# Encoder trunk on one core: last tile of the first scale vector, place of the small transfers, square-root table, zeroing of an accumulator

## The reference

```python
cond = jax.nn.silu(c)
for i in range(DEPTH):
    mod = (cond @ ada_w[i] + ada_b[i])[:, None, :]
    sh1, sc1, g1, sh2, sc2, g2 = jnp.split(mod, 6, axis=-1)
    h = rmsnorm(x, norm_w[i, 0]) * (1 + sc1) + sh1
    h = gated_deltanet(...) if i % 2 == 0 else conformer_conv(...)
    x = x + (1 + g1) * rmsnorm(h, norm_w[i, 1])
    h = rmsnorm(x, norm_w[i, 2]) * (1 + sc2) + sh2
    h = swiglu(h, ffn_in_w[i], ffn_out_w[i])      # (silu(gate) * up) @ out_w
    x = x + (1 + g2) * rmsnorm(h, norm_w[i, 3])
```

## Time and profile before

| | |
|---|---|
| median of three runs | 3267.35 us (3266.91 to 3268.53) |
| profiled execution, its own time | 3268.26 us |
| its span in the profile | 3266.7 us |
| busy share of the span | TensorE 90%, VectorE 69%, ScalarE 39%, GpSimd 5% |
| mean granted TensorE clock | 0.95 |
| HBM traffic | 730 MB, 224 GB/s over the span |

### The profile page before, as it was taken

The page is one execution under the profiler, slowest core; times in us unless marked ns, Lnnn a source line. Parts: engine busy times, 40 slices in busy tenths (PEclk is TensorE's granted clock), DMA queues, the critical chain, the costliest instruction groups (busy, mean ns, idle before and its releaser), DMA issues.

```text
span 3266.7 us, 37727 instructions
## 1 busy us (share of the span) xinstructions
PE 2953.7 (90%) x13796; PEld 2382.1 (73%) x13796; DVE 2264.2 (69%) x2388; ACT 1275.6 (39%) x1383; POOL 163.6 (5%) x313
## 2 busy tenths in 40 slices
PE   1699999997777698899999999799987999999998
PEld 1577778876777577788888888644576888888886
DVE  6588868967776478787877877529966655555555
ACT  2356634335554334333333333421144333333333
POOL 0011111320111000000000000000000000000000
PEclk8799999998998799999999999899998999999998
DMA  9666766674332598798888888354334766656653
GB/s 376 227 224 238 244 218 217 206 235 146 104 104 65 182 372 327 274 341 308 310 308 315 337 315 333 99 167 149 122 121 155 252 206 216 201 201 203 214 204 122
DMA packets 322173, 731.61 MB, mean 224 GB/s; under 512 B 48128, under 2 KB 64336, under 8 KB 293648
## 3 DMA queue, kind: packets, MB, share of 16 engines
q1 hardware_dynamic: 316256, 709.85, 61.5%
q0 software_dynamic: 5808, 20.35, 1.8%
HBM read 710.45 MB, written 19.69 MB: 224 GB/s over the span
## 4 chain that ended last, share of the span: by engine, by line
PE 82%; DVE 7%; DMA 4%; ACT 3%; issue 2%; POOL 2%; DVEq 0%; SPq 0%; ACTq 0%
PE psg L664 44%; PE psg L670 22%; PE psg L651 5%; DMA aring<-in_ada_w 3%; PE psn L925 2%; PE pst L641 1%; PE psn L691 1%; PE psg L864 1%; DVE wlo L1086 1%; PE psg L885 1%; PE psn L1049 1%; DVE y L1598 1%; PE psn L641 1%; DMA wraw<-in_gdn_out_w 1%; PE pst L856 1%
## 5 line engine op out<-in xcount | busy, mean ns | idle before, releaser
L1722 ACT ACTIVATE whi<-wraw 128x2048 fp32r<-128x2048 f32 x408 | 781.8, 1916 | 1319.7 <-PE psg L670 1163.6
L1086 DVE TENSOR_TENSOR wlo<-wraw,whi 128x2048 fp32r<-128x2048 f32 x408 | 935.2, 2293 | 482.9 <-ACT whi L1722 481.0
L664 PE MATMUL psg<-whi,h_hi 128*128 128x512 f32 x2304 | 731.3, 399 | 33.6 <-DVE h_lo L1678 13.2
L664 PE MATMUL psg<-whi,h_lo 128*128 128x512 f32 x2304 | 719.9, 394 | 0.0
L670 PE MATMUL psg<-wlo,h_hi 128*128 128x512 f32 x2304 | 572.1, 391 | 12.0 <-DVE wlo L1086 12.0
L664 PEld LDWEIGHTS psg<-whi,h_hi 128*128 128x128 f32 x2304 | 435.5, 191 | 127.9 <-issue 25.6
L670 PEld LDWEIGHTS psg<-wlo,h_hi 128*128 128x128 f32 x2304 | 433.6, 188 | 104.0 <-DVE wlo L1086 13.9
L664 PEld LDWEIGHTS psg<-whi,h_lo 128*128 128x128 f32 x2304 | 439.5, 191 | 93.9
L1096 DVE SCALAR_TENSOR_TENSOR aacc<-aring,cond,aacc 128x2048 f32<-128x2048 f32 x150 | 352.0, 2346 | 6.6 <-DMA aring<-in_ada_w 6.0
L651 PE MATMUL psg<-wraw,aring 128*128 128x512 f32 x512 | 221.1, 592 | 0.0
L664 PE MATMUL psg<-whi,g_hi 128*128 128x512 f32 x704 | 219.9, 394 | 0.0
(11 more groups left out here) (251 smaller groups left out, 2600.0 us busy)
## 6 DMA issues: line engine op xcount, KB each, us to landing
aring<-in_ada_w SPq DMA_DIRECT2D x192, 1024.0 KB, 7.0
wraw<-in_ffn_in_w SPq DMA_DIRECT2D x176, 1024.0 KB, 6.8
wraw<-in_gdn_in_w SPq DMA_DIRECT2D x96, 1024.0 KB, 5.1
wraw<-in_ffn_out_w SPq DMA_DIRECT2D x88, 1024.0 KB, 5.2
wraw<-in_cf_pw_w SPq DMA_DIRECT2D x48, 1024.0 KB, 5.5
wraw<-in_gdn_out_w SPq DMA_DIRECT2D x32, 1024.0 KB, 8.5
wraw<-d_rr SPq DMA_DIRECT2D x16, 1024.0 KB, 4.7
x<-in_x SPq DMA_DIRECT2D x2, 2048.0 KB, 9.2
```

The costliest lines, as they stand in the source:

```text
L664: mm(ps[:, t, 0:width], a[:, kc, t * P:(t + 1) * P], wh, start=first and j + n == 0, stop=False)
L1086: tt(wlo[:, j % 2, :], wraw[:, j % 4, :], whi[:, j % 2, :].bitcast(F32), SUB).then_inc(w_lo, 1)
L1722: av(whi[:, j % 2, :], wraw[:, j % 4, :], ACT.Copy).then_inc(w_hi, 1)
```

## The change

Five edits. (1) TensorE first sums `aacc` of the scale (16 matmuls), then multiplies tile 31 into a place of its own in another PSUM bank (16 matmuls); VectorE adds the bias to the first sum and then adds the second. (2) `wba` and `alog` are loaded between the second and third weight tile of qkv, and `gwb` behind the fourth; none stands between the tiles of `ada_w` any more. (3) Factor 1/D and epsilon go into ScalarE's root as its scale and bias; the two VectorE steps and one semaphore wait disappear, and the first half's root comes ahead of the second half's square. (4) `root_table` is a root of one element into `scr` that nobody reads: it stands in front of the last block of a stage, and `out_root` moves in front of the next weight tile's `hi`. At an FFN's end VectorE multiplies blocks 0 to 2 by their weights before block 3 has come. (5) The zeroing of `y` becomes a ScalarE copy with scale 0 behind the third `hi` of the FFN.

```diff
@@ SyncE, opening
             for a in range(4, 2 * KC):
                 load_ada0(a)
-                if a == 16:
-                    for j in range(4):
-                        sp.dma_start(gwb[:, j, :], gdn_norm_w[0].partition_broadcast(P)).then_inc(gw_land, 16)
-                    for n, src in enumerate((gdn_A_log, gdn_dt_bias)):
-                        sp.dma_start(alog[:, n, :], src[0].rearrange("a b -> (a b)").partition_broadcast(P)).then_inc(c_land, 16)
-                if a == 20:
-                    sp.dma_start(wba.rearrange("p (j n) -> p j n", n=P),
-                                 gdn_in[:, QKV + VD:QKV + VD + P].rearrange("(j p) n -> p j n", p=P)).then_inc(wba_land, 16)
...
-            load_qkv(0)
+            for j in range(4):
+                load_w(G_QKV + j, (G_QKV + j) % 4, rows4(gdn_in, j * KT * P, 0))
+                if j == 1:
+                    sp.dma_start(wba.rearrange("p (j n) -> p j n", n=P),
+                                 gdn_in[:, QKV + VD:QKV + VD + P].rearrange("(j p) n -> p j n", p=P)).then_inc(wba_land, 16)
+                    for n, src in enumerate((gdn_A_log, gdn_dt_bias)):
+                        sp.dma_start(alog[:, n, :], src[0].rearrange("a b -> (a b)").partition_broadcast(P)).then_inc(c_land, 16)
+                if j == 2:
+                    load_ada(32, aring, (0, 2), 0)
+            for j in range(4):
+                sp.dma_start(gwb[:, j, :], gdn_norm_w[0].partition_broadcast(P)).then_inc(gw_land, 16)
             load_qkv(1)
@@ TensorE, opening
             for kc in range(KC):
-                if kc == 0:
-                    pe.wait_ge(a0_land[last % 4], 16 * (last // 4 + 1))
-                i = mm(psn[:, 0, kc:kc + 1], aring0[:, last % 4, kc * P:(kc + 1) * P], cond[:, KC - 1:KC], start=True, stop=False)
-                if kc == KC - 1:
-                    i.then_inc(a_used, 1)
-                i = mm(psn[:, 0, kc:kc + 1], aacc[:, 1, kc * P:(kc + 1) * P], ones[:, 0:1], start=False, stop=True)
+                i = mm(psn[:, 0, kc:kc + 1], aacc[:, 1, kc * P:(kc + 1) * P], ones[:, 0:1], start=True, stop=True)
             i.then_inc(a_fin, 1)
+            pe.wait_ge(a0_land[last % 4], 16 * (last // 4 + 1))
+            for kc in range(KC):
+                i = mm(psn[:, 2, kc:kc + 1], aring0[:, last % 4, kc * P:(kc + 1) * P], cond[:, KC - 1:KC], start=True, stop=True)
+            i.then_inc(a_used, 1)
@@ VectorE, pre and post
-                    dve.wait_ge(sq_ok, TT * n + t + 1)
                     r = st[:, 2 * n, t:t + 1]
-                    ts(r, r, 1.0 / D, RMS_EPS, MUL, ADD).then_inc(ms_ok, 1)
                     dve.wait_ge(rt_ok, TT * n + t + 1)
...
-                dve.wait_ge(yr_ok, 3 * n + 1)
-                ts(r, r, 1.0 / D, RMS_EPS, MUL, ADD).then_inc(yr_ok, 1)
                 post_col(n, 3, yb, cw)
@@ VectorE, opening
-            mod_add(2, 1)
+            dve.wait_ge(a_fin, 2)
+            tt(vec[:, NV_C:NV_C + KC], psn[:, 0, 0:KC], vec[:, NV_ADAB + KC:NV_ADAB + 2 * KC], ADD).then_inc(half_ok, 1)
+            dve.wait_ge(half_ok, 1)
+            dve.wait_ge(a_used, 2 * KC)
+            tt(mod[:, 1, :], psn[:, 2, 0:KC], vec[:, NV_C:NV_C + KC], ADD).then_inc(mod_ok, 1)
@@ VectorE, ffn
-                nc.vector.memset(y[:, :, :], 0.0).then_inc(y_zero, 1)
-                dve.wait_ge(y_zero, f + 1)
...
+                dve.wait_ge(y_zero, f + 1)
                 with dve.Fori(0, (GRP - 1) // 2) as i:
...
                     if j == 2:
                         dve.wait_ge(cw_land, 16 * (2 * f + 2))
-                        post_col(2 * f + 1, 0, y, cwb)
-                post_col(2 * f + 1, 1, y, cwb)
-                post_col(2 * f + 1, 2, y, cwb)
+                        for n in range(3):
+                            post_col(2 * f + 1, n, y, cwb)
@@ ScalarE, squares
                 for t in range(TT):
                     act.wait_ge(*ready(t))
-                    if n or t:
-                        act.wait_ge(sq_ok, TT * n + t)
                     av(dump, x[:, t, :], ACT.Square, accum_out=st[:, 2 * n, t:t + 1]).then_inc(sq_ok, 1)
-                for t in range(TT):
-                    act.wait_ge(ms_ok, TT * (n - 1) + t + 1)
-                    av(st[:, 2 * n, t:t + 1], st[:, 2 * n, t:t + 1], ACT.Sqrt).then_inc(rt_ok, 1)
+                    act.wait_ge(sq_ok, TT * n + t + 1)
+                    av(st[:, 2 * n, t:t + 1], st[:, 2 * n, t:t + 1], ACT.Sqrt, scale=1.0 / D, bias=epsr[:, 1:2]).then_inc(rt_ok, 1)
...
+            def root_table():
+                av(scr[:, :], epsr[:, 2:3], ACT.Sqrt)
@@ ScalarE, ahead of FFN 0 (ahead of FFN 1 alike)
             hi(G_F0, G_F0)
+            root_table()
             y_evac(3)
             out_squares(0, 3, yg, dump0[:, :], (ps_read, S_F0))
+            out_root(0)
             hi(G_F0 + 1, G_F0 + 1)
-            out_root(0)
@@ ScalarE, ffn
+                    if j == 2:
+                        av(y[:, :, :].rearrange("p t d -> p (t d)"), ident[:, 0:1].broadcast_to([P, TT * D]), ACT.Copy, scale=0.0
+                           ).then_inc(y_zero, 1)
...
                 hi(gl + 2, g0 + 2)
+                root_table()
                 hi(gl + 3, g0 + 3)
```

More of the change, by code:

```diff
@@ L134, in build @@
         epsr = sb("epsr", [P, 3])
+        scr = sb("scr", [P, 1])
         alog = sb("alog", [P, 2, 64])
@@ L283, in build @@
         xt_ok = sem("xt_ok")
-        wba_land = sem("wba_land")
+        wba_land, half_ok = sem("wba_land"), sem("half_ok")
         ba_done, ba_T, ba_tr = sem("ba_done"), sem("ba_T"), sem("ba_tr")
@@ L290, in build @@
         sq_ok = sem("sq_ok")
-        ms_ok = sem("ms_ok")
         rt_ok = sem("rt_ok")
@@ L1162, in post @@
                 nc.vector.reciprocal(r, r).then_inc(yr_ok, 1)
-                dve.wait_ge(yr_ok, 3 * n + 3)
+                dve.wait_ge(yr_ok, 2 * n + 2)
                 dve.wait_ge(yc_ok, 4 * (n + 1))
@@ L1743, in out_squares @@
                     if n and j + t == 0:
-                        act.wait_ge(yr_ok, 3 * n)
+                        act.wait_ge(yr_ok, 2 * n)
                     av(dump_at, yb[:, t, j * NSL:(j + 1) * NSL], ACT.Square, accum_out=spart[:, t, j:j + 1]
@@ L1748, in out_root @@
             def out_root(n):
-                act.wait_ge(yr_ok, 3 * n + 2)
-                av(st[:, 2 * n + 1, :], st[:, 2 * n + 1, :], ACT.Sqrt).then_inc(yrt_ok, 1)
+                act.wait_ge(yr_ok, 2 * n + 1)
+                av(st[:, 2 * n + 1, :], st[:, 2 * n + 1, :], ACT.Sqrt, scale=1.0 / D, bias=epsr[:, 1:2]).then_inc(yrt_ok, 1)
+            def root_table():
+                av(scr[:, :], epsr[:, 2:3], ACT.Sqrt)
             def pre(n, hi_, hfb, low0):
@@ L2137, in _ @@
             hi(G_F1, G_F1)
+            root_table()
             out_squares(2, 3, y, sg4[:, 0:2, :].rearrange("p a t -> p (a t)"), (ps_read, S_F1))
+            out_root(2)
             hi(G_F1 + 1, G_F1 + 1)
-            out_root(2)
             squares(3, lambda t: (x_up, 5 + t))
```

## The result

The changed kernel takes 3300.03 us (median of 4 runs, 3292.81 to 3303.36) where the one before takes 3267.75 (median of 4 runs, the three of the table above among them). The ratio is 1.0094, 95% interval 1.0082 to 1.0107. 3240.3 was predicted, with a range from 3236 to 3249. The profiled execution took 3299.4 us, span 3297.7.

What follows compares the result with a forecast made beforehand. TensorE was taken to bound the kernel, with 82% of the chain of waits. Gains in the opening, before and in the FFNs, before pw1 and at the end sum to 27.1 us, giving 3240.3, range 3236 to 3249.

Steps and rivals of the forecast that it cites:

- the first one: Whole kernel: TensorE holds 82% of the chain of waits, so only edits where it waits count, shifting later work forward.
- Opening: Stream of `ada_w` tiles: moving small transfers behind the weights gains 8.7 us, tile 31 on its own 0.1.
- Into FFN 0: Before FFN 0: 2.0 us from leaving the stage earlier, 1.7 from the norm's second root starting earlier.
- Into pw1: Before pw1: 0.8 us from leaving the FFN earlier, 1.7 from the norm's second root starting earlier.
- Into FFN 1: Before FFN 1: same code as before FFN 0, 2.0 us from leaving the stage and 1.7 from the norm.
- Waits for `wlo`: TensorE's one wait in each FFN goes once zeroing leaves VectorE: 3.3 us in FFN 0, 3.0 in FFN 1.
- Clock behind the wait: FFN 0: eight products after the wait take 3.45 instead of 2.12 at clock 0.50; 1.3 us regained, least sure.
- End: End of the last FFN: VectorE's blocks 0 to 2 move into TensorE's last tile, gaining 0.8 us.
- Bytes only: Rival, opening: small rows cost only their bytes, the ring of four starves otherwise; gain 3.3, 3245.7 us, chance 0.12.
- The wait comes back: Rival, FFNs: TensorE waits for a later `wlo`, losing 3.3 + 1.3 + 3.0; 3247.9 us, chance 0.08.
- The clock: Rival, restarts: TensorE stays longer at clock 0.50, about 4 us a tile; ten tiles give 3280, chance 0.02.
- Nothing measurable: Rival: the same slow clock after restarts, with six tiles, gives 3264 us; chance 0.02.

Runs made afterwards that it cites:

- without the shift: Changed kernel with `scr` as the fourth column of `epsr`, so no address differs from the kernel before: 3242.29 us, ratio 0.9924.
- first experiment: Kernel before plus one unused tensor (`pad`) behind `epsr`, moving the stationary operands by 32 bytes: 3327.03 us, ratio 1.0189.
- three copies with a good distance: Kernel before with everything behind `wraw` moved by 32 (3268.55 us) or 128 bytes (3266.44), or only what lies behind `epsr` by 256 (3267.75).

## Why the prediction was wrong

**The step that failed** is the first one: "everything gained there should shift all later work forward, since nothing else in the kernel depends on absolute time". It took the pace of TensorE's 9792 split matmuls for given. The change altered it, by a line that stands in the diff and that the sum never priced: the tensor `scr`. Its term was missing, not mis-sized: 27.1 were to be gained and 58 to 65 were lost. 58 is the difference of the medians (3300.03 - 3242.29), 65 the 408 tiles at 0.16; the 7 between them are not settled, and single runs scatter by as much (the two profiled executions differ by 63.1 in their spans). A part is that slower matmuls shorten TensorE's waits for VectorE: those for `wlo` are 4.6 in the changed kernel and 5.7 without the shift. In the mere shift of the kernel before (first experiment) it is 61.

**The mechanisms priced were right.** Measured in the profile after, and for the clock in that of the version without the shift, against the earlier trace rows:

| Term | Predicted | Measured |
|---|---|---|
| Opening | 8.8 | 8.9 |
| Into FFN 0 | 3.7 | 3.6 (12.79 of idle before the norm's transposes, now 9.16) |
| Into pw1 | 2.5 | 2.5 (from the three norms' 9.8) |
| Into FFN 1 | 3.7 | 3.7 (16.52, now 12.82) |
| Waits for `wlo` | 6.3 | 6.3 (3.34 and 2.97, both gone) |
| Clock behind the wait | 1.3 | 1.5 (3.45 at a granted 0.50, now 1.98 at 1.00) |
| End | 0.8 | 0.8 |

The sum is 27.3; the medians give 3267.37 - 3242.29 = 25.1, with an interval of 19 to 31 by that of the ratio. That the median lies 2.0 from the prediction is finer than the four runs can tell (3236.26 to 3246.54), so that closeness is partly luck; the places above are the firmer agreement. Without the shift the `wlo` waits fell by 6.3 (12.0 to 5.7), just these two; the 7.4 of the changed kernel hold 1.1 of the slower matmuls.

**The term of the clock** is nevertheless no constant. The kernels derived from the one before all have the wait in FFN 0 (2.9 to 3.4 us), and the eight products behind it took 3.78, 3.59, 3.01, 3.78, 2.14, 2.63, 2.12, 2.11 and 3.14 in the nine of them, in the order of the runs here. Counted to the next tile's eight, as above, the losses are 2.7, 1.6, 1.6, 2.8, 0.1, 1.8, 0.15, 0.1 and 1.6, and 1.5 in the kernel before (6.92 instead of 5.44). In FFN 1 two of nine took 3.4 to 3.5, the others 2.1. One such row, with the whole wait and next to no loss (everything moved by 128):

```profile
1333.86 2.12 PE L671 MATMUL psg<-wlo,h_hi 128*128 128x512 f32 x8 [3.35 <-DVE wlo L1087]
```

The prediction took one execution's 1.3 for the kernel's; between executions it is 0.1 to 3.0. The Trainium skill (TensorE: Matmul & The Clock Gate, section "Part 1: The HAM clock gate") says that the slow stretch differs from run to run for the same kernel. These rows fit it: the kernel before and its three copies with a good distance have the same instructions and the same wait, and lose 1.5, 1.8, 0.15 and 0.1. What the change really buys here is that there is no wait left behind which the clock could fall: in all five profiled executions without it, with and without the shift, the third tile's eight take 1.98 to 2.03.

**The rivals.** *Bytes only* falls: the two idle times came back with the transfers, 9.0 at the scale's `mod` against the 3.3 of their bytes, and the ring of four was not starved, with four loads under way in the hole. By the packet surcharge of the Trainium skill (DMA: Bandwidth & Descriptors, section "Why small descriptors are slow (HBM only)") the transfers would be worth an estimated 3.9; this trace does not agree, so the surcharge is not the whole price of `gwb`, `alog` and `wba` in that place. No run moved the three one by one; by the rows above the hole in the larger idle time, 6.55, opens behind `gwb` and `alog`, and the 3.20 stand behind `wba`. Why the hole comes is not known. *The wait comes back* falls by the third tiles, at 1335.91 and 2542.16, neither with a wait. *The clock* fell by 0.950 and 0.953; as the one rival with a slower ending it had its mechanism and its place wrong, and its 0.02 was all the weight given to a loss. *Nothing measurable* falls with the interval of the result.

**What I could have seen.** The diff names the tensor, and all stationary operands of the split matmuls are created behind it. No row of the trace before shows what an address costs, so no price could be had from it. The Trainium skill (SBUF — State Buffer, section "Operand start alignment") asks that an operand start at a multiple of its element size, and adds that this is about legality, not speed, and that nothing was timed; it gives no price either. But bounding a new tensor's cost like that of any operation the trace does not show would have widened the range to the slow side.

## What to carry to other kernels

A new tensor is part of a change's cost: look at what it moves in SBUF, and put small scratch into space that is already taken. When matmuls get slower with the same instructions and the same granted clock, compare the median of one source line and the distance from tile to tile, and then add an unused tensor to the old kernel; that one run separates placement from order. Keep the distance between the stationary and the moving operand of fp32r matmuls like these at a multiple of 256 bytes, and when a faster version is measured, test it once with its addresses as they were.

## What the runs showed of the hardware

**Operand distance.** For matmuls with 128x128 stationary and 128x512 moving operands, both fp32r, the pace depends on the distance of the two operands' addresses in a partition: 5.44 us for 24 matmuls (389 ns median) at remainder 0 by 256, 5.60 (396) at 32 and 224, 5.58 (393) at 128. The tile distance at 128, from the changed kernel with `scr` of 32 columns:

```profile
2519.16 2.03 PE L672 MATMUL psg<-wlo,h_hi 128*128 128x512 f32 x8
2524.74 2.02 PE L672 MATMUL psg<-wlo,h_hi 128*128 128x512 f32 x8
```

The absolute address did not matter (both operands moved by 32 or by 128: ratios 1.0005 and 1.0003). The fp32 products kept their median of 592 ns in every run, although in most of them the one operand (`aring`) moved by 32 to 256 and the other (`wraw`) did not. The cause inside the chip is open. That the reads of the two operands disturb each other would fit, since it is their distance that counts, but this is only argued. Remainders of 160 and 192, other sizes and bf16 were not tried.

**Zeroing by a repeated column** on ScalarE, 4096 columns at 3.62, costs what a plain copy costs and 0.15 more than VectorE's memset of 3.47, whose 0.80 of issue time ahead of it goes too.
